# Other orders at five joints of a two-layer encoder kernel, and 28 turns of the identity that nobody reads

## The reference, cut to what matters

```python
def half_ffn(x, i, n):
    h = 0.5 * (silu(x @ w1[i, n]) * (x @ w3[i, n])) @ w2[i, n]
    return layer_norm(ALPHA * x + h)

def layer(x, i):
    x = half_ffn(x, i, 0)
    m = pool_mixer(x) if i == 0 else stick_breaking(x)   # pooling: trailing means, a matrix per group, a scale
    x = layer_norm(ALPHA * x + m)
    x = half_ffn(x, i, 1)
    gate = sigmoid(x @ w_gate[i] + b_gate[i])
    return layer_norm(ALPHA * x + gate * (p[i] @ w_proj[i]))
```

## Time and profile before

| | us |
|---|---|
| median of three executions | 2460.12 |
| the profiled execution | 2462.4 |
| its span, first to last instruction | 2460.7 |

### The profile page before, as it was taken

The page is one execution under the profiler, slowest core; times in us unless marked ns, Lnnn a source line. Parts: engine busy times, 40 slices in busy tenths (PEclk is TensorE's granted clock), DMA queues, the critical chain, the costliest instruction groups (busy, mean ns, idle before and its releaser), DMA issues.

```text
span 2460.7 us, 38823 instructions
## 1 busy us (share of the span) xinstructions
PE 2419.9 (98%) x15440; PEld 2172.7 (88%) x15440; DVE 1653.7 (67%) x2163; ACT 1097.8 (45%) x1770; POOL 449.0 (18%) x387
## 2 busy tenths in 40 slices
PE   8999999999999999999999999999999999999998
PEld 8999999889999998999999988777776899999986
DVE  6766666787666676886667662666666886666667
ACT  5433343254433343653344343666665443344343
POOL 3221113112111110221111101212223321121100
PEclk9999999999999999999999999999999999999999
DMA  4322232223222223132232225777876132222221
GB/s 137 108 72 78 86 89 91 61 68 113 77 79 86 86 97 95 37 119 86 77 91 90 78 71 165 211 189 211 229 202 182 49 115 86 86 86 86 85 91 68
DMA packets 376643, 259.16 MB, mean 105 GB/s; under 512 B 10321, under 2 KB 339025, under 8 KB 376464
## 3 DMA queue, kind: packets, MB, share of 16 engines
q1 hardware_dynamic: 371360, 239.64, 33.5%
q0 software_dynamic: 5104, 17.04, 2.1%
HBM read 248.22 MB, written 8.42 MB: 104 GB/s over the span
## 4 chain that ended last, share of the span: by engine, by line
PE 91%; DVE 4%; ACT 2%; issue 2%; DMA 1%; POOL 0%; SPq 0%; DVEq 0%; ACTq 0%; POOLq 0%
PE ps L2604 81%; PE ps L806 6%; PE ps L838 2%; PE ps L2653 1%; DVE x L2017 1%; DVE ring L1940 1%; DMA raw<-in_ffn_w_dram 1%; DVE x L2003 1%; DVE small L1958 1%; PE ps L914 0%; ACT e_buf L1627 0%; ACT ring L1374 0%; ACT xt_hi L1397 0%; ACT wt L1652 0%; DVE s_sum L2354 0%
## 5 line engine op out<-in xcount | busy, mean ns | idle before, releaser
L2604 PE MATMUL ps<-xt_hi,ring 128*128 128x320 f32 (+2 forms) x3328 | 784.2, 311 | 8.0 <-ACT xt_lo L1407 3.8
L2604 PEld LDWEIGHTS ps<-xt_hi,ring 128*128 128x128 f32 x3328 | 570.7, 189 | 18.9 <-issue 8.4
L2604 PE MATMUL ps<-ring,h_hi 128*128 128x512 f32 x1760 | 554.1, 391 | 2.2 <-DVE x L2003 1.7
L1940 DVE TENSOR_TENSOR ring<-raw,ring 128x1024 fp32r<-128x1024 f32 (+1 forms) x318 | 435.6, 1375 | 131.4 <-ACT ring L1374 131.1
L2604 PE MATMUL ps<-xt_lo,ring 128*128 128x320 f32 (+2 forms) x1664 | 515.1, 310 | 0.0
L2604 PE MATMUL ps<-s_ops,ring 128*128 128x320 f32 x3168 | 505.9, 309 | 0.0
L2604 PEld LDWEIGHTS ps<-s_ops,ring 128*128 128x128 f32 x3168 | 474.7, 188 | 0.8 <-issue 0.7
L2604 PEld LDWEIGHTS ps<-ring,h_hi 128*128 128x128 f32 x1760 | 331.6, 188 | 73.3 <-DVE x L2003 2.9
L1374 ACT ACTIVATE ring<-raw 128x1024 fp32r<-128x1024 f32 (+1 forms) x318 | 286.9, 931 | 238.2 <-PE ps L2604 211.9
L1160 POOL TENSOR_TENSOR t_buf<-raw,t_buf 128x512 f32<-128x512 f32 x88 | 114.2, 1298 | 1337.8 <-DVE t_buf L1953 1337.8
L2604 PE MATMUL ps<-ring,h_lo 128*128 128x512 f32 x880 | 343.9, 391 | 0.0
(11 more groups left out here) (202 smaller groups left out, 2494.1 us busy)
## 6 DMA issues: line engine op xcount, KB each, us to landing
raw<-in_ffn_w_dram SPq DMA_DIRECT2D x264, 512.0 KB, 3.9
k_raw<-in_cache_k_dram SPq DMA_DIRECT2D x128, 256.0 KB, 4.9
v_raw<-in_cache_v_dram SPq DMA_DIRECT2D x128, 256.0 KB, 4.3
raw<-in_sb_w_in_dram SPq DMA_DIRECT2D x24, 512.0 KB, 5.3
raw<-in_ple_w_gate_dram SPq DMA_DIRECT2D x16, 512.0 KB, 3.8
g_b<-in_ln_g_dram POOLq DMA_DIRECT2D x8, 512.0 KB, 5.6
b_b<-in_ln_b_dram POOLq DMA_DIRECT2D x8, 512.0 KB, 7.0
raw<-in_sb_w_out_dram SPq DMA_DIRECT2D x8, 512.0 KB, 5.4
```

The source lines that it names most:

```text
L1940: ve.tensor_tensor(ring[:, slot, 1, col:col + cols], conversion_source(u), ring[:, slot, 0, col:col + cols].bitcast(F32), ALU.subtract).th ...
L2604: return pe.matmul(out, w, xx, start=first, stop=last, skip_group_check=True)
```

## The change

**Begin.** `hi` and `low` of x2 and the conversion of the first gate unit are cut in halves of 512 columns, which alternate; `product1(0)` waits for the first halves (semaphores `third_lo`, `gate0_split`), `product2(0)` for the second ones. Behind the three turned tiles TensorE turns the identity 18 times (`idle_turns`).

**End of FFN 0.** VectorE scales the first pool unit before the ten results and the second one before the third tile is normalised; the splits stand behind the third and the fourth tile. ScalarE converts unit 0 first and takes `hi` of x0 before the conversion of unit 1.

**Ends of FFN 1, 2, 3.** The first unit of the next stage is converted before the last silu (ScalarE) and before the last hidden product (VectorE), the second before the ten results, the third at the third tile.

**Pooling.** TensorE turns x2 before it subtracts x1, then turns the identity 10 times; ScalarE takes the square root of the third tile before `low` of x0 and takes x2 in halves; VectorE subtracts these halves around the statistics of the fourth tile.

**v, out, embed.** The table of exponentials is loaded at the third value tile, not at the first. In the out stage x2 is turned two chunks earlier and subtracted before the last chunk; ScalarE takes its `hi` before the fourth square root. In the embed stages `hi` of x4 stands before the second sigmoid. At the end of the last one the fourth tile is centred and its first half rescaled before the last bias is added, its second half right behind it.

**Last pair.** Upper and lower parts of three `suffix` steps are set apart by other work of TensorE; two conversions move.

The diff, cut to its core:

```diff
@@ ScalarE and VectorE, halves of x2 and of the first gate unit
+            def third_tile_hi(st, b):
+                k = st.piece["x2"][0]
+                se.wait_ge(piece_full, k)
+                se.activation(half_operand(st, b, 0), half_source(st, b), ACT.Copy
+                              ).then_inc(piece_hi if b else third_hi, 1)
...
+            def first_gate_lo(b):
+                half = slice(b * HK, (b + 1) * HK)
+                ve.wait_ge(*((w_hi_done, 1) if b else (gate0_hi, 1)))
+                ve.tensor_tensor(ring[:, items[0].slot, 1, half], conversion_source(0)[:, half],
+                                 ring[:, items[0].slot, 0, half].bitcast(F32),
+                                 ALU.subtract).then_inc(w_split if b else gate0_split, 1)
@@ ScalarE, load stage (VectorE alike)
                     hi(st, 0)
                     hi(st, 1)
-                    cvt_to(1)
-                    hi(st, 2)
+                    third_tile_hi(st, 0)
+                    first_gate_hi(0)
+                    third_tile_hi(st, 1)
+                    first_gate_hi(1)
@@ ScalarE, end of an FFN
+                if st.next.kind != "pool":
+                    cvt_to(st.next.u0 + 1)
                 silu_of_second(st, FC - 1)
                 hidden_hi(st, FC - 1)
...
+                    cvt_to(first + ahead // 2)
+                    deviation(st, 0)
+                    deviation(st, 1)
+                    hi(st, 0)
                     if ahead == 2:
-                        deviation(st, 0)
-                        cvt_to(first + 1)
-                        deviation(st, 1)
-                        cvt_to(first + 2)
+                        deviation(st, 2)
+                        cvt_to(first + ahead)
+                        low(st, 0)
                     else:
-                        cvt_to(first + 1)
-                        deviation(st, 0)
-                        cvt_to(first + 2)
-                        deviation(st, 1)
-                    hi(st, 0)
-                    cvt_to(first + min(ahead, 3))
-                    low(st, 0)
-                    deviation(st, 2)
+                        cvt_to(first + 3)
+                        low(st, 0)
+                        deviation(st, 2)
@@ ScalarE, last pair, out, last embed, pool, v
-                    if last:
-                        cvt_to(first_out + 2)
...
+                    if last:
+                        cvt_to(first_out + 3)
                     sample_rows(i, 8)
...
+                    if i == PAIRS - 2:
+                        cvt_to(first_out + 2)
...
+                    hi(st, 2)
                     deviation(st, 3)
-                    hi(st, 2)
...
-                        if t < 3:
+                        if t < 3 or t == 3 and st.then == "none":
                             sigmoid(TILES + t + 1)
...
                     hi(st, 0)
+                    deviation(st, 2)
                     low(st, 0)
-                    deviation(st, 2)
                     hi(st, 1)
+                    third_tile_hi(st, 0)
+                    low(st, 1)
+                    third_tile_hi(st, 1)
                     quarter_rounded(st)
-                    hi(st, 2)
-                    low(st, 1)
...
-                        if n == 0:
+                        if n == 2:
                             se.preload_act_table_set("natural_log_exp_and_others")
@@ VectorE, end of an FFN
                 cvt_to(unit["U", (LAST, 3)] + 1)
+                if st.next.kind != "pool":
+                    cvt_to(st.next.u0 + 1)
                 hidden_of_second(st, FC - 1)
...
+                    if ahead == 2:
+                        scaled(first)
+                    else:
+                        cvt_to(first + 2)
                     for j in range(TILES):
                         evacuate_down(st, LAST, 2 * j)
                         evacuate_down(st, LAST, 2 * j + 1)
-                        if j < 3:
-                            cvt_to(first + min(ahead, j + 1 if ahead > 2 else j))
+                        if j == 2:
+                            if ahead == 2:
+                                scaled(first + 1)
+                            else:
+                                cvt_to(first + 3)
                         normalise(st, j)
-                        if 1 <= j <= 3:
-                            low(st, j - 1)
+                        if j == 2 and ahead == 2:
+                            cvt_to(first + 1)
@@ VectorE, last pair, last embed, pool
-                    if last:
-                        cvt_to(first_out + 2)
                     neg_abs(g + 4)
...
                     turned(i, 2, 1)
+                    if last:
+                        cvt_to(first_out + 2)
...
+                    if st.then == "none":
+                        centre(st, 3)
+                        rescale_half(st, 3, 0)
                     add_bias(TILES + 4)
+                    if st.then == "none":
+                        rescale_half(st, 3, 1)
...
                     mix(4)
+                    third_tile_lo(st, 0)
                     spread(3)
-                    low(st, 2)
+                    third_tile_lo(st, 1)
@@ TensorE
+            def idle_turns(count):
+                for _ in range(count):
+                    pe.transpose(ps[:, GATE_BANK, 0:P], ident, ident)
...
-                    suffix(i, 0)
+                    suffix(i, 0, (0,))
                 if i:
                     values(i - 1, 8)
+                if not follows:
+                    suffix(i, 0, (1,))
...
+                    idle_turns(18)
...
-                            if n >= 7 and c == (6 if n == 7 else 4):
+                            if n >= 7 and c == (6, 4, 2)[n - 7]:
                                 turn(st, n - 7)
...
                     turn(st, 1)
+                    turn(st, 2)
                     subtract(st, 1)
+                    pe.wait_ge(x_upd, st.next.y0 - 1)
+                    idle_turns(10)
```

106 lines of the change are left out of this document (75 added, 31 removed).

## The result

| | before | changed |
|---|---|---|
| median of four executions, us | 2460.34 | 2444.81 (2443.77 to 2445.01) |
| the profiled execution, us | 2462.4 | 2444.74 |
| its span, us | 2460.7 | 2443.0 |

The ratio is 0.9933, with a 95% interval of 0.9916 to 0.9950: 15.5 us less, where 20.0 were forecast. The interval stands for 12 to 21 us less; in the group of run 12, with nine executions of the kernel before and five of the changed one, the difference of the medians is 17.2.

A forecast was written before the change was run, and what follows sets the result against it. TensorE's queue was taken as the bound, so only its idle 41 us and half-clock stretches could be won. The terms summed to -20.0 from the median of 2460.12, giving 2440.1; 8 in 10 between 2435.5 and 2447.5, reaching to 2449.

The forecast's parts named there:

- last pair: Last pair of heads: half of 4.8 us idle goes by parting suffix steps and moving a conversion, -2.5.
- out: Out stage: the 1.16 us wait for `low` on ScalarE shrinks, x2 being turned and subtracted earlier, -1.0.
- behind pooling: `product1(0)` after pooling: about 2.0 of the hole and 1.4 of half clock go, +0.5 for VectorE's later splits, -2.9.
- FFN 0: End of FFN 0: the 5.0 us wait for `hi` of x0 and 2.7 of half clock behind it go, -7.7.
- the stretch in pooling: Half clock at 473.50, 3.20 us busy: worth 1.6 if it goes, half taken, -0.8.
- the ends of FFN 1 to 3: These ends, with embed and v: three waits of 0.55, 0.5 from first weights, 0.75 from a table load, -2.9.
- the begin: Start of FFN 0: 4.5 us won at the first product not booked; third gate unit's chain starts 0.36 later, +0.3.
- Rival A: VectorE or the transfers take the FFN 0 gain back: 2.7 there instead of 7.7, 2445 us; chance 0.15.
- End of the kernel: After TensorE's last product: VectorE's centring, reciprocal and rescaling of the fourth tile move into idle time, -2.5.
- rival D: Small joints give nothing: last pair, out and FFN ends (2.5 + 1.0 + 2.9) stay out, 2446.5 us; chance 0.09.
- Rival B: Unread turns hold no clock: 1.4 lost behind pooling, nothing at the begin, 2441.5 us; chance 0.14.
- Rival C: Slower: ScalarE's conversion before the last silu waits for its load in three FFNs, 2461 us or more; chance 0.02.

The follow-up runs named there:

- run 12: The changed kernel, unchanged, measured again beside run 11: 2444.01 us, ratio 0.9930.
- run 3: Changed kernel with the end of FFN 0 on ScalarE and VectorE and the end of the kernel put back as before: 2454.56 us, ratio 0.9971.
- run 2: Changed kernel without its 28 unread turns (18 at the begin, 10 behind pooling): 2445.20 us, ratio 0.9935.
- run 6: Changed kernel, begin reordered: GpSimd's first weight differences behind its first sum, second gate unit converted before sums are rounded, split before x's differences: 2444.40 us.
- run 9: Changed kernel with run 6's GpSimd order, VectorE's left x difference before the second unit's split, sums rounded after the left blocks: 2442.37 us.
- run 11: Kernel of run 10, with VectorE's right x difference moved behind the first product sum of the second chunk: 2442.09 us, ratio 0.9921.
- run 1: The kernel before the change, unchanged, profiled once more: 2460.81 us, span 2459.1.
- run 5: Changed kernel with first gate product added before last centring behind pooling, x2 subtracted after out's last chunk, out's third conversion behind last exp and log: 2442.56 us.
- run 10: Changed kernel with the begin of run 9 and the three later moves of run 5: 2442.36 us, ratio 0.9924.
- run 4: Changed kernel with last pair and out stage put back (suffix in one piece, conversions at old places, x2 turned and subtracted late): 2445.31 us, ratio 0.9934.
- run 7: Changed kernel with ends of FFN 1, 2, 3, the exponentials' table load and the embed stages' sigmoid order put back: 2449.61 us, ratio 0.9951.

## Why the prediction was right, and which of its steps were wrong

The time lay in the range and the forecast was within 4.7 us of it. Part of that is luck. By the two traces last pair, out, behind pooling and FFN 0 with the stretch in pooling gave 5.2 us less than forecast (2.0, 1.4, 1.1, 0.7), and the ends of FFN 1 to 3 and the begin 3.0 more (2.5, 0.5), for reasons that have nothing to do with each other. The signs that were named came out: no hole and no 0.50 near 442, `product1(0)` at 11.81 and 488.03 at 1.00, the new wait at 21.54. The bounds as written add up to 2435.0 and 2455.9, not 2435.5 and 2455. By its steps:

**FFN 0, 7.7.** Right: hole and half clock went as worked out, VectorE's moved work fitted, TensorE never waited there. Rival A, with 2.7 instead of 7.7, is refuted by run 3, where 6.5 came back. But the size is 5.0 for the hole and 1.5 to 2.7 for the clock.

**End of the kernel, 2.5.** Right, 2.4 by the traces and 2.4 in run 3.

**Begin, +0.3.** Right in what bounds it, not in how it moves. The head of the chain was to come 0.36 later and came 0.5 earlier, and GpSimd's first sum, 0.5 longer beside VectorE's difference of weights (12.78 to 14.55), took that back; the 0.5 us that shorter operations of VectorE might have won were not seen. Where the head stands differs from one execution to the next: `copy_quarters` starts at 11.91 in run 12, of the same kernel. Over the seven profiles of changed kernels with this order of the begin the third unit's products start between 29.20 and 29.71, in the two of before at 28.95 and 29.41. That this chain is the bound: run 2 changes the first product and not the third unit's, runs 6, 9 and 11 move the third unit's by giving its chain another order. The new hole was 2.44, forecast 3, and it did bring half clock, which the forecast had only as its upper bound. It cost nothing, since even so TensorE arrived 0.22 early; in run 3 that half clock is missing, TensorE waits 1.35 for the third unit and starts it at 29.58.

**Half clock as a constant.** This is the step that failed. I booked 0.8 for the stretch inside pooling and 1.4 for the one behind it as if they belonged to the program. The second is missing in run 1, where nothing was changed; held against run 1, the step behind pooling is 0.5 instead of 1.8. The first is there in 9 of the 14 profiles made of these kernels and absent in 5 (runs 2, 3, 5, 10 and 12), at different places between 456 and 477, with and without the change. It follows as well that "the profiled run lies 2.3 above the median" was no constant to carry over. 1.3 of that surplus was the stretch behind pooling. The two profiles are 17.7 us apart, with run 1 in place of the first 16.1. That the executions near the median of before lack the stretch is likely and not shown: their mean granted clock is 0.995 or 0.996, that of the profiled one 0.994, and which stretch that is can be read from a trace alone.

**Behind pooling, 2.9, and out, 1.0.** Mechanism half right. The first product came 1.8 and 0.7 earlier than the work ahead of it explains, and behind pooling the clock gave 1.2 more, but another chain starts at the same place: the last tile's result, its normalisation on VectorE and the first product sum. I had it as a wait of 0.5 behind pooling and not at all behind out. Measured 1.2 (0.95 of it at one wait) and 1.15 came back. Behind pooling VectorE's split took 2.05 instead of 1.23, beside GpSimd's lower parts; behind out the subtraction of x2 now stands ahead of the last chunk and delays that tile by 0.45. Run 4 shows the zero, run 5 that one wait stands right behind the other.

**Last pair, 2.5.** Wrong in size: 0.5. The waits for GpSimd's lower part and for VectorE's keys went as forecast, but TensorE then waited 1.08 and 0.87 at the next steps for ScalarE: for the copy of the keys, and for the sample rows, ahead of which it now makes a conversion. Only the second is shown to be its cause: with the conversion moved back in runs 5 and 11 the 0.87 is gone and 0.2 to 0.3 us are won; in run 11 the 1.08 stays. Nine holes of 4.6 us in all before are nine of 4.7 now. I took half of an idle sum without asking who would be late next. This and out are where rival D was right, 3.4 us of its 6.4.

**Ends of FFN 1 to 3, 2.9.** Too low: 5.4 by the traces, 4.7 in run 7. Besides the three waits of 0.55 there were three for `hi` at the next stages' begins (0.45, 0.75 and 0.45 in the trace of before), and all three went whole; I had priced those places through other rows, and the remaining steps of 0.1 to 0.4 not at all.

**Rival B** (turns hold no clock) is refuted at the begin by run 2, 0.66 without and 1.00 with them over the first products, and by the turns' own pace. TensorE at the start of run 9:

```profile
4.81 5.35 PE L2743 MATMUL ps<-ident_r,x 128*128 128x128 f32 x24 [4.81 <-DVE mask_r L2519]
9.96 2.37 PE L2798 MATMUL ps<-ident_r 128*128 128x128 f32 x18
```

The first turns start 0.21 us apart, those from 10.5 on 0.11 us apart, and TensorE had done nothing but turns until then: they raise the clock as well. The Trainium skill, "TensorE: Matmul & The Clock Gate", "Part 4: PE-mode transpose", says that the full rate doesn't engage for transposes; here it did, and the measurement decides. Behind pooling the turns won nothing (run 2), so the 1.4 us that B put there were never theirs. **Rival C** never arose: the conversion ahead of the last silu waited for no load that TensorE noticed.

## What to carry to other kernels

A half-clock stretch in one profile can be a draw: the one behind the 5.0 us hole at the end of FFN 0 was there in all three profiles with that hole, but twice as long in two as in the third; the one behind 2.6 us in one of two; the one inside pooling in 9 of 14. Look at it in a second execution before booking it, and book the hole in front of it alone. A hole filled is worth what is left after the next chain that starts at the same event; follow that chain (here VectorE's, through the last tile) to its own wait before taking the gain. Where several in-order queues share a start, moving one step early (run 6) gives nothing until the step ahead of it in each of the other queues is moved as well (runs 9, 11).

## What the runs showed of the hardware that I had not expected

Unread turns of the identity kept the clock at 1.00 across 18 of them in 2.13 us, and a hole of 0.82 behind them; a hole of 2.40 without them brought 0.50, one of 1.13 behind pooling did not. The length of the hole alone doesn't decide it: 2.44 at 21.5 brought 0.50, 2.72 at the same place in run 3 and 2.62 behind pooling in run 1 did not.

GpSimd's addition of 256 columns took 0.73 or 1.6 to 1.7 us by what VectorE did. In run 11, GpSimd and VectorE:

```profile
19.32 0.74 POOL L1197 TENSOR_TENSOR sums<-sums 128x256 f32<-128x256 f32 x1
...
21.28 1.60 POOL L1201 TENSOR_TENSOR sums<-sums 128x256 f32<-128x256 f32 x1
```

```profile
19.33 0.47 DVE L2207 TENSOR_TENSOR tmp<-ps,tmp 128x320 f32<-128x320 f32 x1
...
20.53 1.76 DVE L1977 TENSOR_TENSOR ring<-t_buf,ring 128x1024 fp32r<-128x1024 f32 x1
```

Beside an operation that reads PSUM it is short, beside one that reads two operands from SBUF it is long, and that one is long as well (1.76 instead of 1.21 at 28.04, with GpSimd idle). That agrees with the Trainium skill, "SBUF — State Buffer", "SBUF: two separate sides": with two SBUF inputs the two engines lock each other out of a shared port pair.
